# Two-layer RWKV-7 / Conformer model with a hybrid third block: how six norm totals are summed, and what the products around them read

## The reference

```
for layer in (0, 1):
    h = rmsnorm(x);  x += rwkv7_time_mix(h) if layer == 0 else conformer_conv(h)
    x += memory_cross_attention(rmsnorm(x), memn)        # q, kv, xo products
    x += conv_ffn(rmsnorm(x))                            # up, width-3 conv, silu(gate)*val, down
x = rmsnorm(x)                                           # final_norm_g
x += gated sum of GLA and forgetting attention of rmsnorm(x)   # in2, branch, out2
x += conv FFN of rmsnorm(x)                              # up2, down2
return rmsnorm(x)
rmsnorm(x) = x * rsqrt(mean(x*x, features) + 1e-6) * g
```

## Time and profile before

| | us |
|---|---|
| median of 3 runs | 2588.29 |
| the runs | 2571.11, 2588.29, 2600.59 |
| the profiled execution | 2581.97 |
| its span, first to last instruction | 2580.2 |

### The profile page before, as it was taken

How to read it: one execution, slowest core, us unless ns; L and a number is a source line. 1 busy time by engine, 2 the same in 40 slices (tenths; PEclk the granted TensorE clock), 3 DMA queues, 4 the chain that set the end, 5 groups by cost and what they waited for, 6 DMA issues and landing times.

```text
span 2580.2 us, 62015 instructions
## 1 busy us (share of the span) xinstructions
PE 2489.3 (96%) x25266; PEld 2350.5 (91%) x25266; DVE 1362.2 (53%) x2058; ACT 1135.1 (44%) x1677; POOL 994.1 (39%) x488
## 2 busy tenths in 40 slices
PE   7999998999999999998999999999999999999998
PEld 6888885997999999877979999999998769999998
DVE  7666554514577731898434777612143345555521
ACT  8834445544444432335434433433244444444422
POOL 3333220561444454424423444444443104444442
PEclk8999999999999999998999999999999999999999
DMA  4221001341222333313312223233222102322332
GB/s 152 79 74 44 1 1 64 111 168 47 90 93 97 98 115 108 113 58 115 98 49 79 85 98 98 97 100 114 90 91 73 50 1 90 98 98 98 98 101 72
DMA packets 62181, 219.44 MB, mean 85 GB/s; under 512 B 6752, under 2 KB 9184, under 8 KB 61408
## 3 DMA queue, kind: packets, MB, share of 16 engines
q1 hardware_dynamic: 58880, 207.76, 24.7%
q10 hardware_dynamic: 3168, 9.75, 1.1%
HBM read 213.29 MB, written 4.19 MB: 84 GB/s over the span
## 4 chain that ended last, share of the span: by engine, by line
PE 82%; DVE 8%; issue 6%; ACT 3%; POOL 1%; DVEq 0%; DMA 0%; POOLq 0%; ACTq 0%
PE psum L589 69%; DVE psum L2748 5%; PE psum L735 3%; PE psum L743 2%; PE psum L1094 1%; PE psum L1043 1%; PE psum L1276 1%; POOL wl L536 1%; PE psum L1315 1%; DVE psum L2319 1%; ACT wh L1408 1%; ACT psum L1438 0%; PE psum L1278 0%; PE psum L705 0%; PE psum L1082 0%
## 5 line engine op out<-in xcount | busy, mean ns | idle before, releaser
L536 POOL TENSOR_TENSOR wl<-raw,wh 128x1024 fp32r<-128x1024 f32 x388 | 948.0, 2452 | 1442.5 <-ACT wh L1408 1442.4
L589 PE MATMUL psum<-upl,wh 128*128 128x256 f32 x3696 | 736.0, 281 | 14.2 <-DVE upl L2839 7.4
L1408 ACT ACTIVATE wh<-raw 128x1024 fp32r<-128x1024 f32 x388 | 407.1, 1056 | 616.6 <-PE psum L589 593.4
L589 PE MATMUL psum<-uph,wh 128*128 128x256 f32 x3276 | 646.5, 279 | 3.9 <-DVE upl L2560 2.3
L589 PE MATMUL psum<-uph,wl 128*128 128x256 f32 x3276 | 644.1, 278 | 0.0
L589 PEld LDWEIGHTS psum<-upl,wh 128*128 128x128 f32 x3696 | 563.3, 189 | 27.6 <-issue 27.0
L589 PEld LDWEIGHTS psum<-uph,wh 128*128 128x128 f32 x3276 | 497.7, 189 | 6.2 <-DVE upl L2560 2.7
L589 PEld LDWEIGHTS psum<-uph,wl 128*128 128x128 f32 x3276 | 496.2, 189 | 0.0
L589 PE MATMUL psum<-hidh,wh 128*128 128x256 f32 x1056 | 211.8, 279 | 0.0
L589 PE MATMUL psum<-hidl,wh 128*128 128x256 f32 x1056 | 211.0, 278 | 0.0
L589 PE MATMUL psum<-hidh,wl 128*128 128x256 f32 x1056 | 211.0, 278 | 0.0
(11 more groups left out here) (475 smaller groups left out, 4476.9 us busy)
## 6 DMA issues: line engine op xcount, KB each, us to landing
raw<-in_weights SPq DMA_DIRECT2D x388, 512.0 KB, 3.3
xt<-in_x SPq DMA_DIRECT2D x4, 512.0 KB, 5.5
xt<-in_x ACTq DMA_DIRECT2D x1, 2048.0 KB, 9.1
out_x<-xt SPq DMA_DIRECT2D x6, 256.0 KB, 2.3
mem<-in_mem ACTq DMA_DIRECT2D x1, 1024.0 KB, 10.9
memn<-memh ACTq DMA_DIRECT2D x1, 1024.0 KB, 6.5
memn<-meml ACTq DMA_DIRECT2D x1, 1024.0 KB, 9.8
memh<-memn ACTq DMA_DIRECT2D x1, 1024.0 KB, 4.8
```

What stands on the lines that cost most here:

```text
L536: pool.tensor_tensor(wl[:, s, :], raw[:, s, :], wh[:, s, :].bitcast(F32), ALU.subtract).then_inc(split_done, 1)
L589: ins = pe.matmul(out[:, n:n + HALF], w, m[:, n:n + HALF], start=start and j == 0 and n == 0, stop=stop and j == 2 and n + HALF >= out.sha ...
L1408: act.activation(wh[:, s, :], raw[:, s, :], ACT.Identity).then_inc(split_hi, 1)
```

## The change

For the six norms the total is taken in another way. ACT rounds the sum of squares to fp32r (`sums[:, 0]`, `sum_high`), DVE subtracts to get the rest (`sums[:, 1]`, `sum_low`), and PE adds four fp32r matmuls of 256 columns with fp32r ones (`split_total`) in place of the one plain matmul. `sums` lies where `sq` lies. In five of them the total stands behind the second product tile and no longer behind the first; in `kv0` it stays where it was. The copies `firsth`, `firstl` go, and all up tiles read `uph`, `upl`. `ones` gets a tile of its own, set by DVE. Four tiles get a transpose of the identity (`apart`) ahead of their first product, into the bank that they then overwrite: the first of `xo0` and `xo1`, tile 1 and tile 17 of `in2`. Some loops of `in2`, `q1` and `cin` are written out to fit.

```
@@ -229,6 +229,8 @@
+    for stage in ("norm_x0", "norm_ffn0", "norm_conv", "norm_x1", "norm_ffn1", "norm_ffn2"):
+        plan.take(stage, sums=1)
@@ -262,16 +264,19 @@
-        common = place("common", [P, 3 * P])
+        common = place("common", [P, 2 * P])
+        ones_r = place("ones", [P, P], F32R)
+        sums = at("sums", [P, 2, T], F32R, sq_at)
-        ident, ones, blk64 = (common[:, j * P:(j + 1) * P] for j in range(3))
+        ident, blk64 = (common[:, j * P:(j + 1) * P] for j in range(2))
+        ones = ones_r[:, :].bitcast(F32)
@@ -619,16 +623,31 @@
-            def tile(stage, j, source, hi, lo, n=T):
+            def apart(t):
+                pe.transpose(bank[t % 4][:, 0:P], ident, ident)
+            def tile(stage, j, source, hi, lo, n=T, behind_plain=False):
+                if behind_plain:
+                    apart(t)
+            def split_total(stage):
+                pe.wait_ge(sum_lo, plan(stage, "sums") + 1)
+                for j in range(2):
+                    for c in range(0, T, HALF):
+                        ins = pe.matmul(bank[4][:, c:c + HALF], ones_r[:, :], sums[:, j, c:c + HALF],
+                                        start=j == 0 and c == 0, stop=j == 1 and c + HALF == T)
+                ins.then_inc(sum_mm, 1)
@@ -659,10 +678,11 @@
+            pe.wait_ge(ones_ready, 1)
-                pe.matmul(bank[b][:, 0:3 * P], ones, common[:, :], start=True, stop=True)
-                pe.matmul(bank[b][:, 3 * P:T], ones, ident, start=True, stop=True)
+                pe.matmul(bank[b][:, 0:2 * P], ones, common[:, :], start=True, stop=True)
+                pe.matmul(bank[b][:, 2 * P:T], ones, common[:, :], start=True, stop=True)
@@ -1030,7 +1050,7 @@
                 dense("kv0", "norm_mem0", memh, meml, n=MEM, units=4)
-                norm_total("norm_x0")
+                split_total("norm_x0")
                 dense("kv0", "norm_mem0", memh, meml, n=MEM, units=12, skip=4)
@@ -1061,9 +1081,11 @@
+                    tile("q1", 1, "norm_x1", headh, headl)
-                    norm_total("norm_x1")
-                    dense("q1", "norm_x1", headh, headl, units=4, skip=1)
+                    split_total("norm_x1")
+                    for j in range(2, 5):
+                        tile("q1", j, "norm_x1", headh, headl)
@@ -1094,18 +1116,18 @@
-                dense(f"xo{l}", f"heads{l}", headh, headl)
+                tile(f"xo{l}", 0, f"heads{l}", headh, headl, behind_plain=True)
+                for j in range(1, KT):
+                    tile(f"xo{l}", j, f"heads{l}", headh, headl)
-                norm_total(norm)
-                pe.wait_ge(first_hi, KT * (l + 1))
-                pe.wait_ge(first_lo, KT * (l + 1))
-                for j in range(1, 3):
-                    tile(up, j, norm, firsth, firstl)
-                dense(up, norm, uph, upl, units=2 * FT - 4, skip=3)
-                tile(up, 2 * FT - 1, norm, uph, upl)
+                tile(up, 1, norm, uph, upl)
+                split_total(norm)
+                dense(up, norm, uph, upl, units=2 * FT - 4, skip=2)
+                for j in range(2 * FT - 2, 2 * FT):
+                    tile(up, j, norm, uph, upl)
@@ -1128,9 +1150,9 @@
                 tile("cin", 0, "norm_conv", acth, actl)
-                norm_total("norm_conv")
-                dense("cin", "norm_conv", acth, actl, units=4, skip=1)
-                for j in range(5, 8):
+                tile("cin", 1, "norm_conv", acth, actl)
+                split_total("norm_conv")
+                for j in range(2, 8):
                     tile("cin", j, "norm_conv", acth, actl)
@@ -1159,7 +1181,10 @@
                     dense("in2", "norm_h", acth, actl, units=n, skip=skip)
-                inner(1, 12)
+                tile("in2", 1, "norm_h", acth, actl, behind_plain=True)
+                inner(2, 8)
+                for j in range(10, 13):
+                    tile("in2", j, "norm_h", acth, actl)
                 pe.wait_ge(evacuated, t0 + 13 + UC)
@@ -1176,7 +1201,10 @@
                               stop=True).then_inc(z_mm, 1)
-                inner(17, 8)
+                tile("in2", 17, "norm_h", acth, actl, behind_plain=True)
+                inner(18, 4)
+                for j in range(22, 25):
+                    tile("in2", j, "norm_h", acth, actl)
                 def gate(n):
@@ -1487,7 +1515,12 @@
-            def deltas_normed(stage, per, norm, gain=None, h=acth, again=None):
+            def sum_high(stage):
+                act.wait_ge(sq_used, plan(stage, "sq") + KT + SC)
+                act.activation(sums[:, 0, :], rstd[:, :], ACT.Identity).then_inc(sum_hi, 1)
+            def deltas_normed(stage, per, norm, gain=None, h=acth):
@@ -1510,11 +1543,6 @@
-                        if again:
-                            act.wait_ge(hi_ready, i * 4 + (g0 + s + 1))
-                            hold()
-                            act.activation(again[:, i * 4 + s, :], h[:, i * 4 + s, :].bitcast(F32),
-                                           ACT.Identity).then_inc(first_hi, 1)
@@ -1523,6 +1551,8 @@
                         half(i)
+                if not gain:
+                    sum_high(norm)
             def last_deltas():
@@ -1800,6 +1830,7 @@
                 squares("norm_x0", k, x(k))
+            sum_high("norm_x0")
@@ -1879,7 +1910,7 @@
                         act.activation(headh[:, j, :], tmp[:, (g0 + j) % 2, :], ACT.Identity).then_inc(hi_ready, 1)
-                deltas_normed(f"xo{l}", 1, f"norm_ffn{l}", h=uph, again=firsth)
+                deltas_normed(f"xo{l}", 1, f"norm_ffn{l}", h=uph)
             def ffn(l):
@@ -2190,6 +2221,7 @@
+            dve.memset(ones_r[:, :].bitcast(F32), 1.0).then_inc(ones_ready, 1)
@@ -2234,7 +2266,12 @@
-            def residual_normed(stage, per, norm, gain, acc, col=0, h=acth, l=actl, bias=None, again=None):
+            def sum_low(stage):
+                dve.wait_ge(sum_hi, plan(stage, "sums") + 1)
+                dve.tensor_tensor(sums[:, 1, :], rstd[:, :], sums[:, 0, :].bitcast(F32), sub).then_inc(sum_lo, 1)
+            def residual_normed(stage, per, norm, gain, acc, col=0, h=acth, l=actl, bias=None):
@@ -2260,9 +2297,6 @@
-                        if again:
-                            dve.wait_ge(lo_ready, i * 4 + (g0 + s + 1 + SC))
-                            dve.tensor_copy(again[:, k, :], l[:, k, :].bitcast(F32)).then_inc(first_lo, 1)
@@ -2270,6 +2304,8 @@
                         half(i)
+                if n == 1:
+                    sum_low(norm)
             def residual_last():
@@ -2588,6 +2624,7 @@
                 squares_added("norm_x0", k)
+            sum_low("norm_x0")
             def attention(l):
```

More of the change, by code:

```diff
@@ L91, in constants @@
     f = lambda m: m.astype(np.float32)
-    common = np.concatenate([f(s == t), np.ones((P, P), np.float32), f(same64)], 1)
+    common = np.concatenate([f(s == t), f(same64)], 1)
     tt = np.arange(64)[None, :]
@@ L121, in constants @@
     }
-CONST_COLS = {"c_common": 3 * P, "c_prep": 4 * 8, "c_core": 7 * CH, "c_post": 5 * P,
+CONST_COLS = {"c_common": 2 * P, "c_prep": 4 * 8, "c_core": 7 * CH, "c_post": 5 * P,
               "c_hybrid": T + 2 * P + 8 * P}
@@ L357, in build_program @@
         cu = place("cu", [P, 4, T + 2])
-        firsth, firstl = (at("first" + n, [P, KT, T], F32R, zone + 49504 + 16384 * j) for j, n in enumerate("hl"))
         assert act_at % 512 == 32 and zone % 512 == 192
@@ L443, in build_program @@
         mid_split = sem("mid_split")
-        first_hi, first_lo = sem("first_hi"), sem("first_lo")
+        sum_hi, sum_lo, ones_ready = sem("sum_hi"), sem("sum_lo"), sem("ones_ready")
         x_ready = sem("x_ready")
@@ L2169, in hybrid @@
                         sigmoids(2 * k + 6, 2 * k + 8)
-                deltas_normed("out2", 1, "norm_ffn2", h=uph, again=firsth)
+                deltas_normed("out2", 1, "norm_ffn2", h=uph)
             def last_norm():
@@ L2661, in attention @@
                 head_lows(3)
-                residual_normed(f"xo{l}", 1, f"norm_ffn{l}", ["norm_ffn_g"], [rstd], l * KT, uph, upl, again=firstl)
+                residual_normed(f"xo{l}", 1, f"norm_ffn{l}", ["norm_ffn_g"], [rstd], l * KT, uph, upl)
             def ffn(l):
@@ L3014, in hybrid @@
                     lows("branch", yh, yl, i)
-                residual_normed("out2", 1, "norm_ffn2", ["norm_ffn_g_2"], [rstd], 0, uph, upl, again=firstl)
+                residual_normed("out2", 1, "norm_ffn2", ["norm_ffn_g_2"], [rstd], 0, uph, upl)
             def ffn2(scaled):
```

## The result

| | before | after |
|---|---|---|
| median, us (9 runs each) | 2583.37 | 2608.62 |
| lowest and highest | 2565.45, 2600.59 | 2605.26, 2613.58 |
| profiled execution, its span | 2581.97, 2580.2 | 2608.97, 2607.1 |

The change makes the kernel **slower** by about 1%: ratio 1.0106, 95% interval 1.0074 to 1.0138. The forecast was 2568. Rival B, an fp32r total that breaks the pace, gave 2610 and a chance of 0.08; its mechanism is what happened in the FFNs.

A forecast was written before the change was run, and what follows sets the result against it. PE bounds the kernel, running the same matmuls at two paces. From the profiled 2581.97 us, −1.5 −14.4 −1.28 +0.8 −1.0 +0.2 +3.3 = −13.9 gave 2568 us; own range 2562 to 2575, wider range 2560 to 2592.

The forecast's parts named there:

- Rival B: FFNs, behind the second tile: the fp32r total breaks the pace as the plain one did; 2610 us, chance 0.08.
- item 2: up1, down1: first tile, total and the other 63 tiles get faster, gain 14.4 us, if the stretch is fast.
- Item 1: up0 and up2: total with second and third tile goes from 12.06 to 11.33 us, gain 1.5 for both.
- Item 3: xo1 at the pace of xo0 gains 1.28 us; four lone transposes at 0.2 each lose 0.8.
- Item 4: q1: total and four tiles go from 0.46 + 22.99 to 22.45 us, gain 1.0.
- Item 5: kv0: PE waits 1.4 us more behind the total, fast half tiles return 1.3; net loss 0.2.
- Item 6: cin and convolution: DVE's chain starts 2.8 us late, plus 0.5 for the clock; loss 3.3, bounds 1.5 and 5.
- Item 7: All stages with copies: the copies that go and the new rounding lie under product tiles, counted at nothing.
- A: xo1 and the FFN behind it: a lone transpose does not make xo1 fast, one stretch stays slow; 2583, chance 0.2.
- C: Whole kernel: paces have nothing to do with totals and copies; a loss of 3, 2585, chance 0.07.

The follow-up runs named there:

- experiment 1: The changed kernel, but PE adds up no total in the three FFN norms (ACT takes each partition's own sum): 2568.53 us, one run.
- experiment 2: The changed kernel, with the ones of the three FFN totals at 0 modulo 512 bytes, sums still at 192: 2567.59 us, one run.
- experiment 4: The changed kernel, with ones and sums of the FFN totals both at 0 modulo 512 bytes: 2606.62 and 2610.48 us, ratio 1.014.
- experiment 6: The changed kernel, with tiles 2 and 3 of each up product reading the copies firsth, firstl again: 2567.73 us, ratio 0.9982.
- experiment 3: The changed kernel, with ones of the FFN totals still at 192 modulo 512 bytes, sums at 384: 2607.53 and 2609.23 us, ratio 1.014.
- experiment 11: The kernel before, with transposes ahead of xo0 and xo1, no odd copies, each plain FFN total computed twice in a row: 2610.41 and 2614.86 us, ratio 1.0187.
- experiment 12: The kernel before, with transposes ahead of xo0 and xo1, fp32r totals in FFNs and q1, FFN ones at 0, no copies: 2561.02 us, ratio 0.9984.
- experiment 9: The kernel before, with a transpose ahead of xo0 and xo1 and without the odd copies: 2605.07 and 2608.59 us, ratio 1.0164.
- experiment 10: The kernel before, without odd copies or transposes, plain ones of the FFN totals at 0 modulo 512 bytes: 2604.91 and 2607.63 us, ratio 1.0162.

## Why the prediction was wrong

**The step that failed** is in item 2: "After the change nothing plain stands between the transpose ahead of `xo` and the end of `down`, so `xo1` decides." It took the plain form to be the only thing that disturbs a pace. `xo1` did come out fast, and tiles 0 and 1 of `up1` too, but the four fp32r matmuls of the new total started the slow pace themselves. Experiments 1 and 2 show it: without the total, or with its ones elsewhere, 5.440 us a tile. Item 1 leaned on the same assumption without saying so: it took the 64 tiles of `up0` and `up2` behind the new total to stay fast. The size of the error is three slow FFNs of 13.6 us each, 40.8 us, where 2608.6 less 2568 is 40.6; one of the three was paid before as well.

Point by point, by the items:

- **Item 1** (up0 and up2, −1.5): the total took 0.48 us in place of 0.45, and the 64 tiles behind it were slow, +12.9 and +12.8. Rival B had 13.6 for the tiles; that less the 0.7 of item 1 is what was measured.
- **Item 2** (−14.4): −0.7. The shorter total and the fast first tiles came, the 13.4 did not.
- **Item 3** (−1.28 for `xo1`, +0.8 for four transposes): `xo1` gave 1.55. A lone transpose costs 0.03 us to the next start and the tile behind it has 5.57 or 5.58 where others have 5.49; in `before` the tile behind the head products costs that and more, so the transposes gained. The 0.2 each was too dear.
- **Item 4** (−1.0): `q1` has 16.47/3 = 5.49 a tile and is 1.02 us shorter, as forecast (half of it is gone by the end of the attention behind it), though its total has the same two places as those of the FFNs. The tiles of `cin` and `q1` hold two feature tiles from `act_odd`, those of the FFNs none. Those stages are fast behind the fp32r total in all fifteen cases traced, in two of which (`q1` in experiments 4 and 6) PE came to it slow; that the odd feature tiles are why is an inference.
- **Item 5** (`kv0`, +0.2, bounds −1.5 and 1.5): +1.45. The chain of waits was right. ACT, DVE and POOL in the kernel after:

```profile
505.30 2.43 DVE L2609 TENSOR_TENSOR rstd<-rstd,sq 128x512 f32<-128x512 f32 x1 [1.79 <-ACT sq L1810]
...
507.76 0.63 ACT L1521 ACTIVATE sums<-rstd 128x512 fp32r<-128x512 f32 x1 [2.49 <-DVE rstd L2609]
508.29 0.37 ACT L1859 ACTIVATE keys<-psum 128x256 f32<-128x256 f32 x1
...
509.68 2.39 POOL L540 TENSOR_TENSOR wl<-raw,wh 128x1024 fp32r<-128x1024 f32 x1 [2.51 <-ACT wh L1436]
```

  Less the 2.3 us by which this execution was late already, the evacuation stands at 505.99 (forecast 506.1) and POOL's unit starts at 507.4 and ends at 509.8 (forecast 510.0). The first half tile behind the total starts at 512.31, which less 2.3 is 1.76 us later than before (508.25), where 1.4 was forecast. The 1.3 us set against it did not come: from there to the transposes it is 34.72 us, slow, where it was 543.29 − 508.25 = 35.04. So the item ends at its upper bound, 1.76 − 0.32 = 1.44. PE shows little of the wait, 0.17 us, because the half tile ahead of the total was slow itself: its matmuls are 0.21 us apart from 508.04 to 511.24, at a granted clock of 0.50, the lower level of 1.2 GHz, behind a pause of PE of 1.8 us (PE had the same pause before, and stayed at 1.00). In experiments 2 and 6, where the matmuls ahead of the total are 0.11 to 0.12 us apart, PE waits behind the total instead, 1.78 and 1.88 us to the next start.

- **Item 6** (convolution, +3.3): +1.05. ACT and DVE behind the total:

```profile
1057.00 0.69 ACT L1585 ACTIVATE rstd<-psum,par 128x512 f32<-128x512 f32 x1 [5.75 <-PE psum L648]
...
1059.72 0.69 DVE L2765 TENSOR_TENSOR gp<-psum,rstd 128x512 f32<-128x512 f32 x1 [7.46 <-issue]
1060.33 0.68 DVE L2765 TENSOR_TENSOR glu<-psum,rstd 128x512 f32<-128x512 f32 x1
```

  `cin` starts at 1045.35, so the evacuation of its tile 1 is 14.98 us behind it. Before it was 12.2, and item 6 has 2.8 more: right. But DVE, busy 151.97 of the 154 us from 1060 on as it was before, set the means up 169.0 us behind the start of `cin` where it had needed 167.7. So 1.45 of the 2.8 us had come back inside the stretch, and another 0.3 by the start of `cout`. The same 230 DVE instructions stand in both stretches, and two places make the difference: one instruction that took 1.88 us in the trace before and 0.75 in this one (1.1 us; its two lines stand last below, the first of them from the trace before), and one step near 1147 us in the trace before, 0.3 us longer there. A busy share counts an instruction that takes longer as busy, and so it hid this slack; why the instruction took longer is open. The extra 0.5 for the clock did not come: from 1214 to 1240, at PE's pause, it was 0.84 where it had been 0.82.

```profile
1060.00:1214.00 154.00, 149.16 (x1030) 125.43 (x1028) 151.97 (x230) 55.53 (x99) 66.97 (x28) 1.00 0.29 96
1214.00:1240.00 26.00, 18.29 (x115) 15.41 (x116) 16.30 (x27) 19.01 (x30) 4.65 (x2) 0.84 0.13 41
```

```profile
1054.24 1.88 DVE L2733 SCALAR_TENSOR_TENSOR gp<-gp,par,glu 128x512 f32<-128x512 f32 x1
1073.82 0.75 DVE L2770 SCALAR_TENSOR_TENSOR gp<-gp,par,glu 128x512 f32<-128x512 f32 x1
```

- **Item 7** (copies and rounding at nothing): held. Outside `kv0` and the convolution only the first attention is longer, by 0.4 us, and that was not followed up.

**The rivals.** B had the place (behind the second tile), the size of a slow FFN and the sum (2610). That its sum comes within 2 us is in part luck: it also held the 3.3 of item 6, 2.25 too much, and half of item 4 as lost, and the 2.3 us by which this execution was late from the start make up for that. It was given 0.08 because fp32r matmuls of mixed places keep a fast pace in `q0`; those are tiles of a product, and experiments 2 to 4 show that no such rule carries over to a total. A is excluded: `xo1` was fast. C is excluded by experiments 1 and 2, which differ from the change in the total alone and gain 40 us. The Trainium skill, "TensorE: Matmul & The Clock Gate", section "Back-to-back issue gap", gives an isolated warm matmul of 256 columns 262 cycles, which is 109 ns at 2.4 GHz, and for streams of weight load and matmul, as here, about 81 ns at 128 columns and 131 at 512, with no figure at 256 and one pace for each width. The rows have 113.3, 116.7 (copies) and 117.8 ns at the same granted clock of 1.00, and the step from the first to the last is what 40 of 2600 us hang on. The measurement decides.

The weakest place of the working was that the evidence on fp32r and place was of one kind only, tiles between tiles. Item 3's bounds were drawn for a price of 0.1 to 0.5 us, while the pace behind the new total, 13.6 us a stage, was left to one sentence.

## What to carry over

Before a long stretch of like matmuls, read the pace on both sides of every foreign instruction, from the starts, not from the busy share: here 0.5 us of a total decided over 13.6 us behind it. An edit that replaces such an instruction should copy the whole address pattern of the instructions around it, weights' side and moving side, and be tried by itself; a form that seems the same is not evidence enough. And where a kernel's runs stand in heaps, look for a state that its stages take over from one another; find the heap of the profiled execution before forecasting against a median.

## What was not expected of the hardware

- A stream of equal fp32r matmuls of 256 columns has two lasting paces, 113.3 and 117.8 ns, at a clock of 1.00, and keeps either over 3000 matmuls, across stages that differ in operand and bank.
- One plain fp32 matmul of 512 columns over all 128 partitions and outputs turned the pace over in 22 of 22 cases, in both directions. Two in a row into one bank with the same operands did not cancel (3 of 3 FFNs of experiment 11); two with different operands into two banks kept the pace, fast or slow. It costs 0.86 us to its successor of the same kind.
- Between the up tiles of the FFNs four fp32r matmuls with both operands at 192 modulo 512 turned a fast pace slow in 3 of 3; at 0 and 192 they kept it in 6 of 6 (experiments 2 and 12). In `cin` and `q1` the same four at 192 left the fast pace in 15 of 15, and in `kv0` slow in three traces (the change, experiments 2 and 3) and fast in three (1, 4 and 6).
- In the slow case a total's own matmuls are slow as well: 116 to 121 ns each, but for one of 112 or 113 in each total of experiment 4. In `cin` and `q1` they are as slow, though fast tiles follow, so they do not foretell the pace.
- With one transpose ahead of it `xo` is fast in every trace that has it (eleven, two stages each), and without it slow in 3 of 6; behind a total the transpose gives three fast FFNs in some executions only (4 of 10 runs by their times).
- Open: the rule of places; why two plain totals in one bank don't cancel and other pairs do; why `xo` comes out of attention at either pace; and why the first tile of `cin` is slow behind the slow `down0` in experiment 9 and fast in experiments 10 and 11, at the same code around it.
